# A kernel of two transformer blocks on one NeuronCore: the mixing weights of the first attention as high and low fp32r parts in one product of 64 contracted rows

## The reference

```python
alpha = jax.nn.softmax(jnp.stack(lses, axis=0), axis=0)
o_a = jnp.sum(alpha[..., None] * jnp.stack(outs, axis=0), axis=0).reshape(B, S, ATT_OUT_W).astype(x.dtype)
```

## Time and profile before

| | us |
|---|---|
| median of 3 runs | 2085.34 (2084.05 to 2087.31) |
| the profiled execution | 2087.92 |
| its span, from the first to the last instruction | 2086.1 |
| TensorE busy | 2040.1 |
| VectorE busy | 1021.1 |
| ScalarE busy | 769.2 |
| GpSimd busy | 80.0 |
| mean granted clock of TensorE | 0.991 of full speed |

### The profile page before, as it was taken

The page is one execution under the profiler, slowest core; times in us unless marked ns, Lnnn a source line. Parts: engine busy times, 40 slices in busy tenths (PEclk is TensorE's granted clock), DMA queues, the critical chain, the costliest instruction groups (busy, mean ns, idle before and its releaser), DMA issues. The chain is left out here.

```text
span 2086.1 us, 22886 instructions
## 1 busy us (share of the span) xinstructions
PE 2040.1 (98%) x9591; PEld 1654.3 (79%) x9591; DVE 1021.1 (49%) x1353; ACT 769.2 (37%) x1217; POOL 80.0 (4%) x132
## 2 busy tenths in 40 slices
PE   8999999999999999999999999999999999999897
PEld 6899986778787888888888888888888777766566
DVE  4443444434343346643244455555554454856665
ACT  4564551332323323442143222222222214366763
POOL 0000000000000000000000000000000000033431
PEclk9999998999999999999999999999999999999999
DMA  5222122222222232333323333323333435210002
GB/s 201 73 69 81 61 81 71 81 86 81 86 81 81 81 101 89 93 101 101 101 89 94 101 101 91 103 89 101 101 89 94 124 96 160 65 41 21 31 21 61
DMA packets 186422, 181.32 MB, mean 87 GB/s; under 512 B 4816, under 2 KB 162896, under 8 KB 186320
## 3 DMA queue, kind: packets, MB, share of 16 engines
q1 hardware_dynamic: 182832, 172.41, 26.9%
q10 hardware_dynamic: 3488, 7.45, 1.3%
HBM read 173.56 MB, written 4.19 MB: 85 GB/s over the span
## 5 line engine op out<-in xcount | busy, mean ns | idle before, releaser
L878 PE MATMUL bank<-xh,wh 128*128 128x512 f32 x1352 | 549.4, 406 | 0.9 <-DVE wl L1618 0.8
L878 PE MATMUL bank<-xh,wl 128*128 128x512 f32 x1352 | 529.3, 391 | 0.0
L878 PE MATMUL bank<-xl,wh 128*128 128x512 f32 x1352 | 528.7, 391 | 0.0
L1618 DVE TENSOR_TENSOR wl<-raw,wh 128x2048 fp32r<-128x2048 f32 (+2 forms) x154 | 342.2, 2225 | 324.3 <-ACT wh L1167 324.3
L1167 ACT CAST wh<-raw 128x2048 fp32r<-128x2048 f32 (+2 forms) x154 | 285.1, 1854 | 383.6 <-PE bank L878 382.2
L878 PEld LDWEIGHTS bank<-xh,wh 128*128 128x128 f32 x1352 | 254.5, 188 | 61.6 <-issue 9.9
L878 PEld LDWEIGHTS bank<-xl,wh 128*128 128x128 f32 x1352 | 254.7, 188 | 57.5 <-issue 6.9
L878 PEld LDWEIGHTS bank<-xh,wl 128*128 128x128 f32 x1352 | 254.4, 188 | 54.9
L878 PE MATMUL bank<-wh,xh 128*128 128x512 f32 x512 | 214.4, 419 | 4.8 <-DVE xl L2140 4.6
L878 PE MATMUL bank<-wl,xh 128*128 128x512 f32 x512 | 202.0, 395 | 0.0
L878 PE MATMUL bank<-wh,xl 128*128 128x512 f32 x512 | 202.0, 395 | 0.0
(11 more groups left out here) (256 smaller groups left out, 2578.8 us busy)
## 6 DMA issues: line engine op xcount, KB each, us to landing
raw<-in_w_in SPq DMA_DIRECT2D x50, 1024.0 KB, 5.1
raw<-in_a_w_in SPq DMA_DIRECT2D x32, 1024.0 KB, 5.7
raw<-in_w_up SPq DMA_DIRECT2D x16, 1024.0 KB, 5.4
raw<-in_w_down SPq DMA_DIRECT2D x16, 1024.0 KB, 6.0
raw<-in_w_proj_b SPq DMA_DIRECT2D x8, 1024.0 KB, 5.1
raw<-in_a_w_out SPq DMA_DIRECT2D x8, 1024.0 KB, 6.0
raw<-in_w_out SPq DMA_DIRECT2D x4, 1024.0 KB, 5.3
raw<-in_w_kv SPq DMA_DIRECT2D x4, 1024.0 KB, 5.1
```

The lines of the kernel that those rows point to most:

```text
L878: m = e.matmul(o, p, q, start=k == 0 and n == 0, stop=k == K - 1 and n == 2)
L1618: m = e.tensor_tensor(lo, r, hi, ALU.subtract)
```

## The change

The alphas get a buffer of their own, 64 x 2048 of fp32r, in the place of the two score buffers. Its first 1536 columns hold the alphas of the three groups: rows 0 to 3 the high part (rounded to fp32r), rows 32 to 35 the low part, all other rows zero. Its last 512 columns hold `spread`, which now has its ones in row h and in row 32 + h, for 64 rows. One fp32r product with 64 rows contracted then gives high plus low. VectorE clears the alphas and copies `spread` in `mix_log`, after it has signalled "lse", and splits the alphas at the end of `mix_pick`.

```diff
--- before
+++ after
@@ constants
     for h in range(4):
-        spread[h, h] = 1
+        spread[h, h] = spread[32 + h, h] = 1
@@ program
                 lseT = sb("lseT", [48, 128], F32, ph)
+                with ExitStack() as ph2:
+                    alphas = sb("alphas", [64, 4 * S], F32R, ph2)
                 pbuf = [sb(f"pb{i}", [128, 2 * S], F32, ph) for i in range(2)]
...
-    spread = dist[0:4, 1072:1584].rearrange("p (h d) -> p h d", h=4)
+    alpha = alphas[:, 0:1536].rearrange("p (g t) -> p g t", g=3)
+    spread = alphas[:, 1536:2048].rearrange("p (h d) -> p h d", h=4)
@@ tensor: mix
-                e.matmul(bank[:, :], spread[:, h, :], tmp[3 + g][0:4, :], start=True, stop=True).then_inc(
+                e.matmul(bank[:, :], spread[:, h, :], alpha[:, g, :], start=True, stop=True).then_inc(
                     *tell("spread", h, g))
@@ vector: mix_log
             e.tensor_tensor(mx, rden, nmx, ALU.subtract).then_inc(*tell("lse"))
+            w.wait_ge(*told("probs", 11, 0))
+            w.wait_ge(*told("probs", 10, 0))
+            w.wait_ge(*told("dist"))
+            e.memset(alphas[:, 0:1536].bitcast(F32), 0.0)
+            e.tensor_copy(alphas[:, 1536:2048], dist[0:64, 1072:1584]).then_inc(*tell("alpha_zero"))
@@ vector: mix_pick
             for g in range(3):
-                e.tensor_tensor(es[g][0:4, :], es[g][0:4, :], M[0:4, :], ALU.mult).then_inc(*tell("alpha", g))
+                e.tensor_tensor(es[g][0:4, :], es[g][0:4, :], M[0:4, :], ALU.mult).then_inc(*tell("mix_a", g))
+            w.wait_ge(*told("alpha_zero"))
+            for g in range(3):
+                w.wait_ge(*told("mix_a", g))
+                e.tensor_copy(alpha[0:4, g, :], es[g][0:4, :]).then_inc(*tell("mix_hi", g))
+                w.wait_ge(*told("mix_hi", g))
+                e.tensor_tensor(alpha[32:36, g, :], es[g][0:4, :], alpha[0:4, g, :], ALU.subtract).then_inc(*tell("alpha", g))
```

## The result

The changed kernel took 2082.56 us (median of 14 runs, 2079.89 to 2084.25); the kernel before, timed beside it, 2087.7 (14 runs, 2084.05 to 2091.45). The ratio is 0.9971, 95% interval 0.9964 to 0.9978: faster by 4.6 to 7.5 us (5.1 us between the two medians), where 9.9 us and a time of 2075.4 (2072.8 to 2079.2) were forecast. The direction was right, the size and the time were not. Three of the before's 14 runs were known at the time of the forecast, with a median of 2085.34; over all of them it is 2.4 us higher. The profiled execution took 2080.95 us (span 2079.1; before 2087.92 and 2086.1), 7.0 us less, 1.6 us under the median of its own kernel.

The account below looks back on a forecast made before the run. TensorE, busy 98% of the span, was taken to bound the kernel. Gains of 6.6 + 3.3 + 0 + 0 = 9.9 us off the 2085.34 us median gave 2075.4 us, range 2072.8 to 2079.2.

Parts of the forecast that it names:

- mixings 0 to 2: First three per-head mixings of the attention groups on TensorE: each 0.78 in place of 2.98 us, 6.6 us gained together.
- clock behind them: TensorE behind mixings 1 and 2: the granted clock no longer falls, 3.3 us gained, bounds 0 and 3.3.
- mixing 3, decay product's start: Fourth mixing, ahead of retention's decay product: its 2.2 us saved give nothing, TensorE's idle grows from 1.29 to 4.1 us.
- clock at the decay product: TensorE's clock falls within or behind the longer wait, as before: put at 0, bounds 2.1 us gained and 1 lost.
- VectorE's additions: Memset and copy before mix_pick (1.9 us), copies and subtractions after the multiplies (3.6 us): hidden, 0 us.
- Everything behind runs at TensorE's pace and moves up whole: Rest of the kernel behind the mixings: keeps the whole gain, so the same 9.9 us come off the median.
- switch of shape: TensorE at each mixing: 0.1 us more for the switch to other operands, within the 0.78 us per mixing.
- rival A: TensorE's clock still falls behind mixings 1 and 2: gain 6.6 us, 2078.7 us; chance 0.11.
- the chain that eats mixing 3: Tile's end to decay product: ScalarE's silu and cast, VectorE's subtraction and multiply take 5.78 us, which TensorE can't shorten.
- C: Mixings: fp32r products with 64 rows go at the fp32 pace of two passes, 2085.5 us; chance 0.03.
- D: VectorE before mix_pick: memset takes 10.0 us, TensorE waits 8 us at mixing 0, 1.8 us lost, 2087.1 us; chance 0.03.
- B: The 4.1 us wait ahead of the decay product brings no or a shorter clock fall: gain 12.0, 2073.3 us; chance 0.07.

Follow-up runs that it names:

- padded run: Changed kernel with six one-column fp32 products (24 records, as many as the change removed) at the start of TensorE's stream: 0.9952 of before, 2079.13 us.
- 128-row run: Changed kernel with alphas of 128 rows (rows 64 to 127 zero) and the constant's 128 rows: 0.996 of before, 2080.06 us.

## Why the prediction was wrong

The ledger of the two profiled executions, in us gained, from the pass ahead of mixing 0 on, which lay 0.6 us later after (316.42 against 315.82; over all traces it lies anywhere from 314.6 to 317.3):

| step | forecast | traces |
|---|---|---|
| mixings 0 to 2, 18 fp32 records to 9 of fp32r | 6.6 | 3 x (2.98 - 1.09) = 5.7 |
| clock behind them | 3.3 | 3.3 |
| mixing 3, decay product's start | 0 | 0 |
| clock at the decay product | 0 | 0.5 |
| VectorE's additions | 0 | 0 |
| rope product's wait | not in the sum | -2.0 |

With the 0.6 us at the start that is 6.9; the spans differ by 7.0.

- **The step that failed** is the sentence that "Everything behind runs at TensorE's pace and moves up whole". TensorE's place did, by 8.8 to 8.9 us at every product from 376 us up to the rope product, and by 6.9 us behind it; there a transfer sets the pace, and the change moved a fetch of TensorE's own instructions into it. I had counted the removed instructions as time and not as 24 places (12 products, 12 weight loads) in a stream that is fetched in blocks. The padded run shows it: 3.8 back to 1.9 us.
- **Mis-sized: the switch of shape.** I took 0.1 us per mixing for other operands; it is 0.4, shown by the 128-row run, 0.9 us over three mixings. With the 0.6 us at the start this is why the decay product came 1.6 us later than forecast. The pass of fp32r itself was right.
- **The clock** was right in mechanism and, for the pair of traces, in size. The cause that I inferred, 4 of 128 rows in use, was one of two that the trace before allowed (the other is the fp32 type), and the runs with 64 and 4 rows in both types tell them apart. As an average over runs the granted clocks give 2.7 to 4.0 us in all, which is in keeping with 3.3 here and 0.5 at the decay product. Which two mixings bring the falls is chance: the second trace of the kernel before has them behind mixings 0 and 2. The Trainium skill's rule (TensorE: Matmul & The Clock Gate, Part 1), under which idleness drops the clock, gave rival A. The runs decide against that rival: products with few rows brought a fall with no idle.
- **The base.** The forecast subtracted from a median of 3 runs that lay 2.4 us low, which is a third of the 7.2 us between 2075.4 and 2082.56. My own range for the run-to-run part was one fall of the clock; the kernel before alone spans 7.4 us in 14 runs. The range was also narrower than its parts: the unknowns named with it add up to 5.1 us upward (1 + 2.1 + 0.3 + 1.7), which ends at 2080.5 and not at 2079.2. The measured time lies above both.
- **Right:** the chain that eats mixing 3 (5.78 us both times, a wait of 3.6 with a fall of the clock behind it), the memset (1.34 us for 1.4 forecast), the copies (0.41 us for 0.49 forecast; a subtraction 0.68), alpha's last part ready 0.4 us ahead of the first spread product, no wait for any low part. So C and D fall; B falls too, since all five traces with a wait of 3.6 to 4.0 us there had a fall at it.
- **Open:** Of the 4.8 us between the 9.9 forecast and the 5.1 of the medians, 2.0 are the rope product's wait and 0.9 the switch of shape; the rest is not placed. 7.0 us lie between the two profiled executions and 5.1 between the medians. In the second block the clock falls at places that differ from run to run; which part of the rest is chance I can't say.

## What to carry to other kernels

A product that uses 4 of 128 rows is dear twice. It costs the same as a fuller one (12 fp32r products took 3.01 us with 4 rows and with 64), and some 3 us of it halved the clock behind it in 7 of 12 cases here though TensorE was busy. Fill rows, and fill all 128 where the neighbours do, since a different shape cost 0.4 us per group here. When an instruction goes, ask what its finish was waited for (mixing 3 gave nothing until its place on VectorE was moved by one step), and also what its place in the stream was: a removed instruction moves every later block fetch against the transfers that the critical path waits for. For a change of a few tenths of a per cent take the base from many runs.

## What the runs showed of the hardware that was not expected

- Instructions come in packets of 16 KB on a queue of their own: 76 over the span, and 77 when TensorE's stream had 232 records more. A packet that fell 4 to 5 us into four SBUF copies came with a wait for them that was 1.4 to 2 us longer (VectorE's from 6.7 to 8.6 us), one that fell 1.3 us into them with 0.3 us.
- Products with 4 of 128 rows, some 3 us of them and no idle, were followed by a fall of the granted clock in 7 of 12 cases, as long a stretch with 64 rows in none of 6.
- A group of fp32r products with 64 rows between products with 128 costs 0.4 us more than one with 128 rows (1.09 against 0.69 us), though its records are no longer each (0.39 us median in both).
- VectorE rounds 512 fp32 of SBUF to fp32r in 0.36 us on 64 partitions and 0.41 on 4, below the 0.49 us of the one-input row before; a subtraction of that size takes 0.68.
